# First two modulation units by column halves, with early half products of two steps, in a two-layer decoder trunk

## What is computed

```python
cond = silu(c)                                    # (1, 1024)
mod = (cond @ w_ada[l] + b_ada[l]).reshape(b, 9, d)
h = modulate(x, mod[:, 0], mod[:, 1])             # x * (1 + scale) + shift
x = post_norm_residual(x, swiglu(h, w_in, w_out), mod[:, 2], 0.5, ln_g, ln_b)
```

## Time and profile before

| | |
|---|---|
| time of three runs, median (lowest to highest) | 1059.79 us (1058.85 to 1062.68) |
| the profiled execution's own time | 1057.72 us |
| its span, first to last instruction | 1055.9 us |
| TensorE busy | 1017.1 us (96%), 4708 products and transposes |
| VectorE busy | 775.5 us (73%) |
| ScalarE busy | 521.4 us (49%) |
| bytes moved | 265.61 MB, mean 252 GB/s |

### The profile page before, as it was taken

One profiled execution on the slowest core, in us unless ns is written; L12 is line 12 of the kernel. 1 busy time (PEld: TensorE's weight loads), 2 busy tenths in 40 slices (PEclk: granted clock), 3 DMA queues, 4 the chain that ended last, 5 costly groups with the idle time before them and its releaser, 6 DMA issues.

```text
span 1055.9 us, 12357 instructions
## 1 busy us (share of the span) xinstructions
PE 1017.1 (96%) x4708; PEld 826.3 (78%) x4708; DVE 775.5 (73%) x908; ACT 521.4 (49%) x852; POOL 85.7 (8%) x160
## 2 busy tenths in 40 slices
PE   3799999999999999999999999999999899999997
PEld 1588888878888878888778888888878778888885
DVE  7677777788875888777877587777779777645475
ACT  1545444556564744544464644544468655434432
POOL 0011111101000011111100011111110010000010
PEclk9899999999999999999999999999999999999999
DMA  9999899965785399989937499999846638556551
GB/s 362 349 302 328 299 327 294 333 214 178 264 275 161 108 354 314 316 293 310 326 131 251 146 332 317 310 300 318 312 158 224 203 119 279 166 193 195 181 184 40
DMA packets 147490, 265.61 MB, mean 252 GB/s; under 512 B 8424, under 2 KB 98920, under 8 KB 147432
## 3 DMA queue, kind: packets, MB, share of 16 engines
q1 hardware_dynamic: 124448, 182.87, 51.1%
q0 software_dynamic: 20928, 75.53, 21.0%
q10 hardware_dynamic: 2056, 6.42, 2.0%
HBM read 263.75 MB, written 1.05 MB: 251 GB/s over the span
## 4 chain that ended last, share of the span: by engine, by line
PE 70%; DVE 17%; DMA 5%; ACT 4%; issue 3%; DVEq 0%; SPq 0%; ACTq 0%
PE psum L1251 14%; PE psum L1253 14%; PE psum L1252 14%; PE psum L1328 7%; PE psum L1326 7%; PE psum L1327 7%; DVE w_lo L838 5%; DVE acc L870 5%; DMA ada<-in_w_ada 4%; PE psum L1359 1%; PE psum L1286 1%; ACT psum L594 1%; ACT w_hi L504 1%; PE psum L1273 1%; DVE qT L980 1%
## 5 line engine op out<-in xcount | busy, mean ns | idle before, releaser
L838 DVE TENSOR_TENSOR w_lo<-raw,w_hi 128x2048 fp32r<-128x2048 f32 x164 | 371.5, 2285 | 45.0 <-ACT w_hi L504 44.9
L1251 PE MATMUL psum<-w_hi,hT_hi 128*128 128x512 f32 x896 | 356.0, 397 | 4.3 <-DVE w_lo L838 4.1
L1253 PE MATMUL psum<-w_hi,hT_lo 128*128 128x512 f32 x896 | 350.0, 391 | 0.0
L1252 PE MATMUL psum<-w_lo,hT_hi 128*128 128x512 f32 x896 | 349.0, 390 | 0.0
L504 ACT ACTIVATE w_hi<-raw 128x2048 fp32r<-128x2048 f32 x164 | 310.5, 1915 | 0.0
L508 ACT ACTIVATE tmp<-psum 128x256 f32<-128x256 f32 x88 | 33.8, 384 | 345.8 <-PE psum L1253 345.8
L1251 PEld LDWEIGHTS psum<-w_hi,hT_hi 128*128 128x128 f32 x896 | 168.2, 188 | 40.3 <-DVE w_lo L838 4.0
L1253 PEld LDWEIGHTS psum<-w_hi,hT_lo 128*128 128x128 f32 x896 | 168.2, 188 | 36.0
L1252 PEld LDWEIGHTS psum<-w_lo,hT_hi 128*128 128x128 f32 x896 | 168.5, 188 | 32.9
L870 DVE SCALAR_TENSOR_TENSOR acc<-ada,cond,acc 128x1024 f32<-128x1024 f32 x128 | 164.1, 1282 | 39.8 <-DMA ada<-in_w_ada 30.2
L1326 PE MATMUL psum<-w_hi,a_hi 128*128 128x512 f32 x368 | 150.5, 409 | 0.0
(11 more groups left out here) (151 smaller groups left out, 706.0 us busy)
## 6 DMA issues: line engine op xcount, KB each, us to landing
raw<-in_w_ffn_in SPq DMA_DIRECT2D x176, 512.0 KB, 5.2
ada<-in_w_ada POOLq DMA_DIRECT2D x128, 512.0 KB, 5.2
raw<-in_w_ffn_out SPq DMA_DIRECT2D x88, 512.0 KB, 5.8
raw<-in_w_qkv_a SPq DMA_DIRECT2D x24, 512.0 KB, 5.0
raw<-in_w_o SPq DMA_DIRECT2D x16, 512.0 KB, 4.7
ada<-in_w_kv_ada POOLq DMA_DIRECT2D x16, 512.0 KB, 5.0
raw<-in_w_kv_b SPq DMA_DIRECT2D x16, 512.0 KB, 6.2
raw<-in_w_ada SPq DMA_DIRECT2D x4, 1024.0 KB, 14.0
```

The source lines that it names most:

```text
L838: nc.vector.tensor_tensor(lo_of(n), slot_of(n), hi_of(n).bitcast(F32), ALU.subtract)\
L1251: nc.tensor.matmul(dst, s_hi, m_hi, start=start, stop=False)
L1252: nc.tensor.matmul(dst, s_hi, m_lo, start=False, stop=False)
L1253: return nc.tensor.matmul(dst, s_lo, m_hi, start=False, stop=stop)
```

## The change

Units 0 and 1 are read by column halves: pieces 0 to 3 are columns 0 to 511 of both units (four rows of 512 columns each; pieces 0 and 1 of the shift, 2 and 3 of the scale), pieces 4 to 7 are columns 512 to 1023. Pieces 4 to 6 go to the places of 0 to 2 and wait in the SP queue for `staged_used`, piece 7 waits for `acc_steps` 4. The SP order is piece 0, piece 1, identity, x tile 0, chunk 0, piece 2, x tile 1, piece 3, chunk 1, pieces 4, 5, 6, chunk 2, piece 7, chunk 3, and chunk 4 waits for all 16 of VectorE's row steps. Chunks 0 and 1 are now k-tiles 0 to 3 of steps 0 and 1; chunks 2 and 3 are their k-tiles 4 to 7.

TensorE sums pieces 0, 1, 2 and 4 itself (`sum_staged`: 16 plain float32 products each, with a 128 x 128 block of the piece as the stationary operand and one column of `cond` as the moving one, so N = 1), VectorE the pieces 3, 5, 6 and 7 (`start_rows`, rows of 512 columns); three times four N = 1 products against a column of ones (`sum_start`) reduce VectorE's sums over partitions. `turn_unit`, L555 and L1060 are gone for both units. VectorE forms coefficients of k-tiles 0 to 3 after the first half, and modulation goes by halves over both token tiles. Then four groups of 12 products (`half_tile(s, t, 0)`) for steps 0 and 1, both token tiles, run over k-tiles 0 to 3, with `sum_staged(4)` between step 0 and step 1. Products of zeros are 12, 10 and 10 ahead of them and 12 and 10 (`add_nothing`) behind them. `ffn(0)` begins with the four second halves. Step 1's products go to the banks `misc`. The VectorE and ScalarE orders of steps 0 and 1 are rewritten to fit; from step 2 on they are as before, as are the other three feed-forwards and the mixers.

```diff
-START_PRODUCTS = (24, 24)
+START_PRODUCTS = (12, 10, 12, 10)
...
+def half_of(n, half):
+
+    return n + (2 if n < 2 else 1) * half
...
-        USE_ORDER += [IN_PAIR[_f][_s], IN_PAIR[_f][_s] + 1]
+        if _f == 0 and _s < 2:
+            USE_ORDER += [2 * _s, 2 * _s + 1]
+        else:
+            USE_ORDER += [IN_PAIR[_f][_s], IN_PAIR[_f][_s] + 1]
         if 1 <= _s <= STEPS - 3:
...
+            place = (qT, kT, v_sb)[m % 4][:, :, :].rearrange("p a n -> p (a n)") if m % 4 < 3 else raw[:, 4, :]
+            return place.rearrange("p (r n) -> p r n", r=4)
...
+                elif n == 4:
+
+                    sp.wait_ge(acc_steps, 16)
...
+            def load_staged(m):
+                unit_, rows, cols = m // 2 % 2, 4 * (m % 2), m // 4
+                src = ada_view(w_ada[0])[:, rows:rows + 4, D * unit_ + 512 * cols:D * unit_ + 512 * cols + 512]
+                if m == 7:
+                    sp.wait_ge(acc_steps, 4)
+                elif m >= 4:
+                    sp.wait_ge(staged_used, m - 3)
+                if m % 4 < 3:
+                    sp.dma_start(staged(m), src).then_inc(staged_in[m], 16)
...
+                    sp.dma_start(staged(m)[:, 0:2, :], src[:, 0:2, :]).then_inc(staged_in[m], 16)
+                    sp.dma_start(staged(m)[:, 2:4, :], src[:, 2:4, :]).then_inc(staged_in[8 + m // 4], 16)
+
+            def load_first(n):
+
+                load(n, inner_chunk(slot_of(n), w_ffn_in[0, 0], 256 * (n % 2), n // 2))
...
+            load_staged(0)
+            load_staged(1)
+            sp.dma_start(cst[:, 0:P], consts[:, 0:P]).then_inc(cst_in, 16)
+            load_x(0)
+            load_first(0)
+            load_staged(2)
+            load_x(1)
+            load_staged(3)
+            load_first(1)
+            load_staged(4)
+            load_staged(5)
+            load_staged(6)
+            load_first(2)
+            load_staged(7)
+            load_first(3)
             load_ffn(0)
...
+                if f == 0:
+                    silu(f, 0, 0)
+                    silu(f, 0, 1)
+                    split_hi(n + 4)
+                    silu(f, 1, 0)
+                    inner_hi(f, 0, 0)
+                    silu(f, 1, 1)
+                    inner_hi(f, 0, 1)
+                    inner_hi(f, 1, 0)
+                    for c in range(5, 8):
+                        split_hi(n + c)
...
+            split_hi(0)
+            for half in range(2):
+                for t in range(TT):
+                    h_half(0, t, half)
+                if half == 0:
+                    split_hi(1)
+                    split_hi(2)
+            split_hi(3)
...
+            def start_rows(m, sums, first):
+
+                dve.wait_ge(staged_in[m], 16)
+                for r in range(4):
+                    if m % 4 == 3 and r == 2:
+                        dve.wait_ge(staged_in[8 + m // 4], 16)
+                    row = 4 * (m % 2) + r
+                    factor, src = cond[:, row:row + 1], staged(m)[:, r, :]
+                    if first and r == 0:
+                        nc.vector.tensor_scalar(sums, src, factor, None, ALU.mult).then_inc(acc_steps, 1)
+                        continue
+                    dve.wait_ge(acc_steps, {3: 0, 5: 4, 6: 8, 7: 12}[m] + r)
+                    nc.vector.scalar_tensor_tensor(out=sums, in0=src, scalar=factor, in1=sums,
+                                                   op0=ALU.mult, op1=ALU.add).then_inc(acc_steps, 1)
...
+                dve.wait_ge(start_sums, half + 1)
+                cols, sums = slice(4 * half, 4 * half + 4), misc[0] if half == 0 else y[2]
+                nc.vector.tensor_tensor(coef[:, 0, 1, cols], sums[:, 0:4], biasT[:, BIAS_AT[0], cols], ALU.add)
+                nc.vector.tensor_tensor(coef[:, 0, 0, cols], sums[:, 8:12], coef[:, 0, 0, cols], ALU.add)\
+                  .then_inc(coef_ready, 1)
...
+                if f == 0:
+                    inner(f, 0, 0)
+                    inner(f, 0, 1)
+                    split_lo(n + 4)
+                    inner(f, 1, 0)
+                    inner_lo(f, 0, 0)
+                    quarter(0, 1)
+                    inner(f, 1, 1)
+                    inner_lo(f, 0, 1)
+                    inner_lo(f, 1, 0)
+                    split_lo(n + 5)
+                    quarter(1, 0)
+                    split_lo(n + 6)
+                    quarter(1, 1)
+                    split_lo(n + 7)
...
-            for u in range(2):
-                for q in range(4):
-                    accumulate(u, q)
-                    if u == 1 and q == 0:
-                        keep_second_half(0)
-            keep_second_half(1)
...
             dve.wait_ge(rows_ready, 1)
-            dve.wait_ge(second_half_kept, 2)
-            coefficients(0)
-            h_tile(0, 0)
+            own(nc.vector.tensor_scalar_add(coef[:, 0, 0, :], biasT[:, BIAS_AT[1], :], 1.0))
+
             split_lo(0)
-            h_tile(0, 1)
+            start_rows(3, acc[:, 0:512], True)
+            start_coefficients(0)
+            for t in range(TT):
+                h_half(0, t, 0)
             split_lo(1)
+
+            start_rows(5, acc0, True)
+            start_rows(6, acc[:, 512:1024], True)
+            start_rows(7, acc[:, 512:1024], False)
+            split_lo(2)
+            start_coefficients(1)
+            for t in range(TT):
+                h_half(0, t, 1)
+            split_lo(3)
...
+            def half_tile(s, t, half):
+
+                n = IN_PAIR[0][s]
+                pe.wait_ge(w_lo_ready, half_of(n, half) + 1)
+                for k in range(4 * half, 4 * half + 4):
+                    if k % 2 == 0:
+                        pe.wait_ge(h_lo_ready, split_count(0, t, k // 2))
+                    last = three(step_bank(0, s, t), h_tok(k, t), w_half(n, k), k == 0, k == KT - 1)
+                if t == 1:
+                    last.then_inc(w_used, 1)
+                elif half == 1:
+                    last.then_inc(first_tile, 1)
+
+            def sum_staged(m, dst, first):
...
+                pe.wait_ge(staged_in[m], 16)
+                for r in range(4):
+                    row = 4 * (m % 2) + r
+                    for k in range(4):
+                        last = nc.tensor.matmul(dst[:, k:k + 1], staged(m)[:, r, k * P:(k + 1) * P],
+                                                cond[:, row:row + 1], start=first and r == 0 and k == 0, stop=True,
+                                                skip_group_check=True)
+                last.then_inc(staged_used, 1)
+
+            def sum_start(sums, dst):
+                for k in range(4):
+                    last = nc.tensor.matmul(dst[:, k:k + 1], sums[:, k * P:(k + 1) * P], one[:, :],
+                                            start=False, stop=True, skip_group_check=True)
+                return last
+
+            def add_nothing(times):
+
+                for _ in range(times):
+                    nc.tensor.matmul(misc[1], zeros[:, 0:P], zeros[:, :], start=False, stop=False,
+                                     skip_group_check=True)
```

```diff
@@ ffn on TensorE: f == 0 now begins with
+                    for t in range(TT):
+                        half_tile(0, t, 1)
+                    half_tile(1, 0, 1)
+                    turn_inner(f, 0, 0)
+                    half_tile(1, 1, 1)
+                    turn_inner(f, 0, 1)
+                    turn_inner(f, 1, 0)
+                    o = out_chunk(f, 0)
+                    pe.wait_ge(w_lo_ready, o + 1)
+                    inner_done(f, 0, 0)
+                    add_rows(o, inner(0), 0, first=True)
+                    inner_done(f, 0, 1)
+                    add_rows(o, inner(0), 1, first=True).then_inc(w_used, 1)
@@ the start on TensorE
-            turn_unit(0, acc0)
             stay_busy(START_PRODUCTS[0])
-
-            pe.wait_ge(mod_ready, 1)
-            pe.wait_ge(second_half_kept, 1)
-            turn_unit(1)
-            pe.wait_ge(x_in, 16 * TT)
-            turn_x(0, 0)
...
+            pe.wait_ge(cond_ready, 1)
+            sum_staged(0, misc[0][:, 0:4], True)
+            sum_staged(1, misc[0][:, 0:4], False)
+            pe.wait_ge(x_in[0], 16)
+            turn_x(0, 0)
             stay_busy(START_PRODUCTS[0])
+            sum_staged(2, misc[0][:, 8:12], False)
+            pe.wait_ge(x_in[1], 16)
             turn_x(0, 1)
             stay_busy(START_PRODUCTS[1])
+            pe.wait_ge(acc_steps, 4)
+            sum_start(acc, misc[0][:, 8:12]).then_inc(start_sums, 1)
+            stay_busy(START_PRODUCTS[3])
+            for t in range(TT):
+                half_tile(0, t, 0)
+
+            sum_staged(4, y[2][:, 0:4], True)
+            pe.wait_ge(coef_ready, 1)
+            for t in range(TT):
+                half_tile(1, t, 0)
+            pe.wait_ge(acc_steps, 8)
+            sum_start(acc0, y[2][:, 0:4])
+            add_nothing(START_PRODUCTS[2])
+            pe.wait_ge(acc_steps, 16)
```

(27 more changed lines are left out.)

179 lines of the change are left out of this document (84 added, 95 removed).

## The result

The changed kernel took **1076.78 us** (median of 4 runs, 1073.13 to 1077.61) beside 1060.3 us for the kernel before on the same chip: a ratio of **1.0155, 95% interval 1.0127 to 1.0183**. It is slower by 16.5 us, outside the predicted 1050 to 1075; the forecast, 1067 us, was 7.2 us above the median of before. The profiled execution has a span of 1074.7 us against 1055.9, 18.8 us more; I account for that one.

What follows compares the result with a forecast made beforehand. The prediction took TensorE, 96% busy, to bound the kernel. A start 6.6 us later plus 1.0 us of waiting for VectorE, added to the median of 1059.8, gave 1067 us, range 1050 to 1075.

Steps and rivals of the forecast that it cites:

- The price of an N = 1 record: TensorE's one-column sums: each record, a load with its product, costs 0.11 us at full clock, 0.22 at half.
- Rival C: TensorE's sums: N = 1 records almost free, 0.03 us each, transfers then bound; 1050 us (1047 to 1054), chance 0.24.
- The clock in the first sums: TensorE's start: sum_staged(0) and (1) run at half clock and take 14.1 us.
- rival B: First two sums: loads count as work, clock high early, 7 to 9 us not 14.1; 1060 to 1062, chance 0.21.
- Start and stream: TensorE free at 11.0 us, first real product at 39.8, k-tiles 4 to 7 at 61.3: 6.6 us later.
- 43.6: Kernel before: the time in us at which an unbroken product stream would have begun, counted by products already done.
- rival D: Clock falls between real products, around sum_staged(2) and (4), on top of A: 1076 us (1072 to 1080), chance 0.10.
- A: The forecast case: half clock in the first sums, 0.11 us a record at full clock; 1064 to 1072, chance 0.45.
- Late next: Behind 61.3 us, until k-tiles 4 to 7 of step 2: TensorE waits 1.0 us for VectorE, range 0 to 2.
- The later stages: Steps 2 to 10 and all later stages: the same work, TensorE bound, nothing added.
- the sum (7.6): Whole kernel: 6.6 us of later start plus 1.0 us of waiting, added to the median of before.

Runs made afterwards that it cites:

- e2: The changed kernel with two of the four rows of each piece that TensorE sums left out; 1065.11 us, ratio 1.0057.
- e7: The changed kernel with 32 zero products ahead of the identity's wait, in TensorE's idle time; 1070.47 us, ratio 1.0102.
- e12: The changed kernel with rows of units 2 and 3 loaded through four buffers, not two, and nothing else; 1071.93 us, ratio 1.0103.
- e9: e1 with rows of units 2 and 3 loaded through four buffers, not two; 1054.27 us, ratio 0.9946.
- e1: The changed kernel with the row sums all on VectorE, still by column halves, and 24, 12, 12 and 10 zero products; 1059.3 us, ratio 1.0006.
- e6: The changed kernel with only 64 of the 1024 columns of units 2 and 3 loaded and summed; 1068.76 us, ratio 1.0085.
- e3: The changed kernel with VectorE's step 1 order changed: low parts of chunks 6 and 7 ahead of unit 2's second and third quarters; 1077.13 us, ratio 1.0175.
- e8: e1 with high parts of chunks 4 and 5 earlier on ScalarE and the low part of chunk 4 earlier on VectorE; 1059.03 us, ratio 1.0005.
- e4: The changed kernel without any of the 54 zero products; 1073.72 us, ratio 1.0145.
- e11: e1 with only 64 of the 1024 columns of units 2 and 3 loaded and summed; 1050.99 us, ratio 0.9919.

## Why the prediction was wrong, step by step

**The price of an N = 1 record** was right: 0.11 us was taken from the two loads of the earlier trace rows and 0.22 from the ratio of the transposes, 0.109 and 0.214 were measured, and e2 shows that the end follows it. Rival C (almost free, 0.24) falls: it needed under 0.075. The floor for small N that the Trainium skill states (TensorE: Matmul & The Clock Gate, Back-to-back issue gap), some 25 ns, is not the price of these records, which are four times as long at full clock. That the loading of the 128 columns of weights sets it is argued, from the equal 0.11 us of the earlier trace rows; no run changed the number of columns.

**The clock in the first sums** was right in its level (half), and rival B falls. Its reason was only in part: e7 shows that the sums do not merely fail to raise the clock, they lose one that is high.

**Start and stream.** TensorE was free at 11.8 us (forecast 11.0), the first real product came at 40.67 (39.8), k-tiles 4 to 7 at 63.46 (61.3): 2.2 us late, 8.8 and not 6.6 against 43.6. Late were the identity and the bias rows (0.8), 12 zeros that I took at full clock (3.7 instead of 2.9) and the products behind the fourth sum (7.2 until the next sum instead of 5.5, some eight of them at half clock); the first two sums, the other products of zeros and the small sums gave 1.2 back. The half clock there is rival D's mechanism at one of its two places: it was given 0.10 and 9 us on top of A, and took 1.7 in the profiled execution. That the measured 1076.78 us is nearly D's 1076 is luck: most of what lies beyond the forecast has another cause.

**"Late next" is the step that failed.** Waiting behind 61.3 us was put at 1.0 us, range 0 to 2. In the stretch that the step speaks of it measured 5.1: 3.4 of waiting for the low part in step 2 and 1.7 of half clock behind it. With what came later and was put at nothing, it is 9.2. VectorE's own work was estimated well (19 to 22 us for some 20): from 63.46 us to the low part's end at 86.97 it took 23.5 us, 21.4 without the 2.06 us for which it stood. That would have been a wait of 1.3 us, as in e12. What the step left out is that VectorE *stands* for rows in program order; of them the prediction says only that "they are used after `ffn(0)` has begun". With two buffers, GpSimd issues a row only once VectorE has finished the one two before it. The row then landed 5.5 us after its issue (the median of those issued in 56 to 92 us), with the weight chunks under way beside it, and VectorE stood 2.06, 0.54 and 1.80 us in 80 to 91 us, with the low part queued behind the first of these. Nor did the step price what a wait of that length can do to the clock. e12 (5.5 us back by earlier transfers alone), e9 (5.2 us of VectorE's standing in e1 taken away, 6.4 us of time back by the ratios) and e6 (waits of 60 to 110 us gone) show the cause; e3 and e8 show that neither VectorE's nor ScalarE's order alone removes it.

**The later stages** were taken as unchanged ("the same work, TensorE bound"). Of the 9.2 us, 1.7 lie at 102 us, in the wait for `a_lo`, and 2.4 at 237, 411 and 545 us. The later part is not shown to be a price of the change: its largest piece, at 237 us, is absent from e3 and e4. That the late release of transfers is part of the loss (the loads of unit 2's rows and of chunk 4 wait for a count that comes after 50 us, and no transfer runs in 50 to 55 us) is argued, not shown: no run moved it alone.

**What stays open.** 0.8 us of the profiled difference; the waits at 237, 411 and 545 us; and how much of the `a_lo` waits (3.7 us in e12 still) is VectorE's work and how much its order. e6 and e11, which leave work out, shortened them to 1.4 and 1.7, and e8's order to 2.1, with a new wait in their place.

Direction and mechanism of the start were right, then, and of the 11.2 us by which the profiled execution (18.8) passed the sum (7.6), 8.2 are this one term with the later stages, 2.2 the start and 0.8 open.

## What to carry to other kernels

Summing rows with one-column plain float32 products costs two weight loads per product: here 0.22 us a product at full clock and 0.43 at half, so 128 x 512 elements cost 0.9 to 1.7 us on TensorE. One row of that size took 0.48 to 0.80 us on VectorE, an engine that here could have done it earlier (e1). Before pricing an earlier or a later stream, follow the second engine's queue in program order through the next two steps, with each transfer it stands for and the count that releases this transfer: in e1 an earlier start was worth nothing, because a two-deep ring of buffers set the pace behind it. A wait in front of the bound engine can cost more than its length, by the products that run at half clock behind it, here 1.7 us on top of 3.4. It need not: the 3.56 us of the kernel before were followed by a granted clock of 1.00 (46 to 50 us).

## What the runs showed of the hardware that I had not expected

One-column products, issued without a pause, let TensorE's clock fall from 1.00 to 0.50: in e7 at 15.7 us, within the second sum, and after the fourth sum of the kernel after, at 49.9 us for 3.4 us. In or behind the third sum of the kernel after it did not fall. In the profiled executions of e6 and e12, whose TensorE issues the same instructions in the start as the kernel after, it fell within that sum, and k-tiles 4 to 7 began at 67.19 and 67.69 us, not 63.46. In these two, rival D's mechanism was at work at both of its places: one execution's start can differ by 4 us from another's, which is why the comparisons above go by ratios over several runs. This row of e6 shows the third sum, begun at full pace and finished at half:

```profile
31.40 4.67 PE L1445 MATMUL psum<-cond,v_sb 128*128 128x1 f32 x32
```

And the granted clock column reads 1.00 in 10 to 20 us of the kernel after, while the sums there run at the pace of half clock, 0.214 us a record; before the first change it records, that column is no measure. The pace of a known instruction is.
